# Three-pass down tiles throughout, low parts of the gated products on GpSimd, and an earlier schedule of norm, scores and gates

## The chip, the cores and the metric

One NeuronCore of a Trainium2 chip. The metric is the device time of one execution in microseconds; the kernel before was timed three times.

## The reference, cut to what matters

One layer over 640 rows (512 of a prompt, 8 streams of 16), width 1024: `h = rmsnorm(x)`, one projection `h @ w_in` into nine parts, a width-3 convolution branch and a retention branch of four heads, both gated, `x += m @ w_out`; then `h2 = rmsnorm(x)` and a layer of 16384 single-neuron experts:

```python
q = (hb @ w_q).reshape(PEER_BLOCK, PEER_HEADS, 2, D_HALF)
s = jnp.einsum('thpd,pkd->thpk', q, sk)
sv, si = lax.top_k(s, PEER_TOPK)
...
g = jax.nn.softmax(ts, axis=-1)
a = jax.nn.gelu(jnp.einsum('thkd,td->thk', u_tab[e], hb))
out = jnp.einsum('thk,thkd->td', g * a, v_tab[e])
```

and at the end `x += out` and a last norm.

## The kernel before, in words

The program is one core's, written by hand for each engine: every engine has its own list of instructions in program order, and semaphores tie them. TensorE's order is: turn the normalised rows (`turn_rows`, L1561), 72 products of `w_in` tiles (`product`, L1514 to L1516) with the attention of the head before in between, `w_out` (`by_token`), the query tiles (L1710), 128 up tiles of the expert layer (`up`, L1750) and 128 down tiles (`down_three`, L1807 to L1809, or `down`, L1815).

**Rounded passes.** A float32 product is done in three matmuls of a rounded type (high x high, high x low, low x high) where high and low parts have been made. Of a weight tile ScalarE makes the high part (L692) and GpSimd the low part (`low`, L644). Of the first norm's rows VectorE multiplies by the gain (L1007) and rounds (L1008), and GpSimd makes the low part (`rows_low`, L653); there are two buffers `hf`, one for each half of a block of 128 rows, and TensorE transposes into banks 0 and 1 for every block.

**First norm.** ScalarE squares the five blocks of rows (L736), takes one square root for all; VectorE makes the factors (L984 to L989); ScalarE scales each block (L724); TensorE transposes it; VectorE, GpSimd as above.

**Heads and turns.** Beside the products of `w_in` VectorE also transposes all 128 tiles of `u_t` by 32x32 blocks (`turn`, L1032), so that rows of the up table can be gathered later; SP loads each tile and stores it in four pieces, in the same queue as the `w_in` tiles. In `scores` VectorE multiplies five score tiles by their decay (L1056), scales keys and queries, and turns two u tiles before the fourth score tile; in the first head two more ahead of the first.

**Two ways through the experts.** The first 256 rows are done sparsely: for each of their 128 picks per row one up row and one down row are gathered for all 128 partitions by GpSimd's indirect DMA (L679) into 14 slots, VectorE takes the dot (L1375), ScalarE the gelu and the weight (L894, L900), VectorE adds the weighted down row (L1392). Two picks make a pair (`pair_step`), 128 pairs in all, one dot two pairs ahead. The other 384 rows are done densely: up tiles with gelu, stored as `acts`; gates scattered by one-hot products (`scatter`, L1765) into `gates`; both loaded back in groups of four tiles (`group_in`), multiplied by VectorE (`weigh`, L1426) into `p32`, a ring of four.

**What orders the pairs.** VectorE runs `retrieval(tt)` for five blocks with 9 pairs inside each of the last four (INSIDE), GAP pairs between them, pairs beside the gates, BEFORE_DOWNS pairs, and the rest spread over the down tiles (`pair_after`). `pair_at`, EXP_AT, SCORES_AT, PICKT_AT and GATE_AT are up tiles at which ScalarE and TensorE have their share in their own lists.

**Down tiles.** `three(e)` says which tiles go in three passes: all but e % 8 == 7. For those ScalarE rounds the tile (L947) and the gated product (L949), VectorE makes both low parts (`low_of_tile` L1433, `low_of_gated` L1439). The rings of high and low parts are four tiles deep, that of the loaded tiles eight. TensorE does three 128-row blocks by two halves per tile. GpSimd has only the gathers in this stage; a gather waits until its slot's row of 14 entries ago is used.

Of the kernel before, what the change touches and what calls it, by code (L numbers as in the profile page):

```python
# [72 lines left out]
GAP = 11  # L73
# [12 lines left out]
def pair_at(b):  # L86
# [5 lines left out]
    e = RETRIEVAL_AT + 28.6 * turn + (0.5 + 2.0 * i if i < INSIDE else 17.3 + 0.97 * (i - INSIDE))  # L92
# [7 lines left out]
def three(e):  # L100

    return e % 8 != 7
# [95 lines left out]
def build_program(nc, io):  # L198
    ctx = ExitStack()
    with ctx:  # L200
# [177 lines left out]
        xsT_done = sem("xsT_done")  # L378
        h_split = sem("h_split")
# [85 lines left out]
        def _(sp):  # L465
# [118 lines left out]

            for i in range(3 * A_WQ):
                plain_in(i, io["wq"][i % A_WQ, :, :])
# [4 lines left out]
            def group_in(g):  # L591
                if g >= 2:
                    sp.wait_ge(p_ready, (g - 1) * GROUP)
                if g == 0:
                    for i in range(2):
                        sp.wait_ge(gt_stored[i], 16 * (NB // 2))
                for i in range(2):
                    sp.wait_ge(a_stored[i], 16 * (GROUP // 2) * (g + 1))
                src = gates[g, :, :, :]
                sp.dma_start(gr[:, g % 2, :, :, :].rearrange("p b k t -> p b (k t)"), src).then_inc(g_loaded[g % 2], 16)  # L600
                src = acts[g, :, :, :].rearrange("p k t -> p (k t)")
                sp.dma_start(al[:, g % 2, :, :].rearrange("p k t -> p (k t)"), src).then_inc(al_loaded[g % 2], 16)
# [12 lines left out]
            for u in range(GROUP):  # L615
                down_in(u)
                acts_out(NKEY - GROUP + u)
                if u == 0:
                    group_in(0)
            group_in(1)  # L620
# [18 lines left out]
        def _(pool):  # L639
# [27 lines left out]
            for u in range(GROUP):  # L667
                low(A, u, N_W0 + GROUP + u)
            for n, (kind, r_) in enumerate(ORDER):
                if kind == "u" and r_ % P == 0:  # L670
# [11 lines left out]
                ).then_inc(row_in[n % SLOTS], 16)  # L682


        @block.scalar
        def _(act):
# [44 lines left out]
            for tt in range(TT):  # L731
                act.wait_ge(x_loaded[tt], 16)
                if tt >= 3:
                    act.wait_ge(sum_done, tt - 2)
                bank = 2 + 2 * (tt % 3)
# [1153 lines left out]
```

## Time and profile before

| what | us |
|---|---|
| median of 3 runs | 2223.83 (2220.51 to 2227.95) |
| the profiled execution | 2224.73 |
| its span, first to last instruction | 2222.9 |
| TensorE busy | 2166.9 |
| VectorE busy | 1730.2 |
| GpSimd busy | 866.3 |
| ScalarE busy | 592.8 |
| down stage, first to last matmul | 1670.5 to 2213.9 |

The span is that of the slowest core, here the only one. Busy times of engines overlap. A matmul's recorded length is longer than the distance between two starts, since matmuls are pipelined; distances of starts are used for its cost. The granted clock of TensorE was 0.994 in the mean.

### The profile page before, as it was taken

Reading aid. Unit: us, or ns where it says so; the run is one execution under the profiler, and the core shown is the slowest. Engines: PE = TensorE matmul, PEld = TensorE weight load, DVE = VectorE, ACT = ScalarE, POOL = GpSimd, SP = SyncE. Lnnn points to the kernel's source line nnn. Section 1 sums busy time; section 2 is a strip of 40 time slices with the busy share of each in tenths; the row PEclk is TensorE's granted clock in tenths of the full one; section 3 lists DMA queues with packets and bytes.
Section 4 is the critical chain, followed back from the end, with each engine's and each line's share of the span. In section 5 each row is a group of like instructions: output and inputs, shape, how many; then the busy total and the mean of one; then the engine's idle time right before and its main releaser. Section 6 shows DMA issues by size and latency. Waiting matters only on the chain.

```text
span 2222.9 us, 30818 instructions
## 1 busy us (share of the span) xinstructions
PE 2166.9 (97%) x10473; PEld 1692.8 (76%) x10473; DVE 1730.2 (78%) x3244; ACT 592.8 (27%) x1159; POOL 866.3 (39%) x606
## 2 busy tenths in 40 slices
PE   5999999999999999999999999999999999999998
PEld 5989889899998885655565565577767777777776
DVE  3566675667675285988988989999949898888987
ACT  3212222122223111121221211233324333333333
POOL 4322122223333004576675684512114454454540
PEclk9999999999999999999999999999999999999999
DMA  4999899999983367999999999888899999999993
GB/s 161 304 306 320 288 303 307 318 321 312 309 286 143 108 219 304 355 370 412 403 402 412 389 411 413 337 274 289 292 320 393 413 414 414 413 414 414 414 412 141
DMA packets 314151, 735.40 MB, mean 331 GB/s; under 512 B 30368, under 2 KB 163232, under 8 KB 314016
## 3 DMA queue, kind: packets, MB, share of 16 engines
q1 hardware_dynamic: 189792, 439.67, 54.8%
q0 software_dynamic: 73728, 268.47, 30.6%
q10 hardware_dynamic: 50496, 25.59, 3.8%
q8 instruction: 69, 1.13, 0.2%
q14 instruction: 66, 0.54, 0.1%
HBM read 604.04 MB, written 129.57 MB: 330 GB/s over the span
## 4 chain that ended last, share of the span: by engine, by line
PE 61%; DVE 16%; DMA 7%; issue 6%; POOL 6%; SPq 2%; ACT 1%; DVEq 0%; ACTq 0%; POOLq 0%
PE ps L1750 7%; PE ps L1808 7%; PE ps L1807 7%; PE ps L1809 7%; PE ps L1710 6%; POOL b L679 5%; PE ps L1515 5%; PE ps L1514 5%; DMA b<-in_u_t 5%; PE ps L1516 5%; PE ps L1815 4%; PE ps L1765 3%; DVE b L1392 3%; DMA b<-in_peer_v,b 2%; DVE b L1032 1%
## 5 line engine op out<-in xcount | busy, mean ns | idle before, releaser
L1750 PE MATMUL ps<-b,b 128*128 128x384 f32 x2048 | 665.6, 486 | 0.0
L679 POOL DMA_INDIRECT b<-u_rows,b x256 | 367.2, 1434 | 717.3 <-DVE b L1375 517.9
L1750 PEld LDWEIGHTS ps<-b,b 128*128 128x128 f32 x2048 | 386.8, 190 | 263.4
L644 POOL TENSOR_TENSOR b<-b,b 128x1024 fp32r<-128x1024 f32 x80 | 195.1, 2442 | 468.9 <-ACT b L692 464.4
L1514 PE MATMUL ps<-b,b 128*128 128x320 f32 x1152 | 365.0, 317 | 1.6 <-issue 1.6
L1516 PE MATMUL ps<-b,b 128*128 128x320 f32 x1152 | 357.6, 310 | 0.0
L1515 PE MATMUL ps<-b,b 128*128 128x320 f32 x1152 | 357.5, 310 | 0.0
L1392 DVE SCALAR_TENSOR_TENSOR b<-b,b,b 128x1024 f32<-128x1024 f32 x256 | 330.9, 1292 | 28.3 <-DMA b<-in_peer_v,b 11.2
L1375 DVE CUSTOM_DVE_ANT_0 b<-b,b 128x1024 f32<-128x1024 f32 x256 | 312.5, 1221 | 28.4 <-DMA b<-u_rows,b 22.2
L679 POOL DMA_INDIRECT b<-in_peer_v,b x256 | 291.0, 1137 | 88.6 <-issue 78.3
L1032 DVE STREAM_TRANSPOSE b<-b 128x1024 f32<-128x1024 f32 x128 | 156.9, 1238 | 169.3 <-DMA b<-in_u_t 162.7
L1807 PE MATMUL ps<-b,b 128*128 128x512 f32 x672 | 269.5, 401 | 3.3 <-DVE b L1439 3.3
L1808 PE MATMUL ps<-b,b 128*128 128x512 f32 x672 | 263.2, 392 | 0.0
L1809 PE MATMUL ps<-b,b 128*128 128x512 f32 x672 | 262.1, 390 | 0.0
L1514 PEld LDWEIGHTS ps<-b,b 128*128 128x128 f32 x1152 | 218.0, 189 | 3.0 <-issue 1.9
L1515 PEld LDWEIGHTS ps<-b,b 128*128 128x128 f32 x1152 | 217.8, 189 | 1.0
L1516 PEld LDWEIGHTS ps<-b,b 128*128 128x128 f32 x1152 | 217.6, 189 | 0.0
L884 ACT ACTIVATE b<-ps 128x384 f32<-128x384 f32 x128 | 62.3, 487 | 448.8 <-PE ps L1750 427.8
L707 ACT ACTIVATE b<-ps 128x640 f32<-128x640 f32 (+1 forms) x72 | 50.7, 704 | 423.3 <-PE ps L1516 423.2
L1807 PEld LDWEIGHTS ps<-b,b 128*128 128x128 f32 x672 | 126.4, 188 | 34.9 <-issue 8.0
L1808 PEld LDWEIGHTS ps<-b,b 128*128 128x128 f32 x672 | 126.6, 188 | 30.1 <-issue 4.1
L1433 DVE TENSOR_TENSOR b<-b,b 128x1024 fp32r<-128x1024 f32 x112 | 136.4, 1218 | 14.3 <-ACT b L947 12.4
(164 smaller groups left out, 2588.0 us busy)
## 6 DMA issues: line engine op xcount, KB each, us to landing
b<-in_u_t SPq DMA_DIRECT2D x256, 512.0 KB, 5.5
u_rows<-b SPq DMA_DIRECT2D x512, 128.0 KB, 4.3
b<-in_peer_v SPq DMA_DIRECT2D x128, 512.0 KB
b<-in_w_in SPq DMA_DIRECT2D x72, 512.0 KB
b<-in_wq SPq DMA_DIRECT2D x48, 512.0 KB
acts<-b SPq DMA_DIRECT2D x128, 192.0 KB
gates<-b ACTq DMA_DIRECT2D x12, 2048.0 KB
b<-gates SPq DMA_DIRECT2D x32, 768.0 KB
```

The lines of the kernel that those rows point to most:

```text
L644: nc.gpsimd.tensor_tensor(lo[u][:, :], raw[:, u, :], hi[u][:, :].bitcast(F32), ALU.subtract).then_inc(lo_ready, 1)
L679: nc.gpsimd.indirect_dma_start(slots[n % SLOTS][:, :], None, u_rows if kind == "u" else v_rows, bass.IndirectOffsetOnAxis(ap=row_id[:, r_ ...
L1032: nc.vector.transpose(u_turned[i % 3].rearrange("p (n k j) -> p n k j", n=4, k=KT), u_in[i % 2].rearrange("p (k n i) -> p n k i", k=KT, n= ...
L1375: nc.vector.tensor_tensor_reduce(up_row, up_row, h_row[:, r_ // P, :], 1.0, 0.0, ALU.mult, ALU.add, dots[:, r_ // PAIR % LINES, r_ % PAIR: ...
L1392: nc.vector.scalar_tensor_tensor(token_rows, down_row, row_w[:, b % LINES, i:i + 1], token_rows, ALU.mult, ALU.add).then_inc(row_done, 1)
L1514: nc.tensor.matmul(out, wa_hi[u][:, cols], h_hi[:, k, tok], start=(k == 0), stop=False)
L1515: nc.tensor.matmul(out, wa_hi[u][:, cols], h_lo[:, k, tok], start=False, stop=False)
L1516: last = nc.tensor.matmul(out, wa_lo[u][:, cols], h_hi[:, k, tok], start=False, stop=(k == KT - 1))
L1750: last = nc.tensor.matmul(ps[:, e % 4, 0:TD], w[:, k * P:(k + 1) * P], h2[:, k, SD:T], start=(k == 0), stop=(k == KT - 1))
L1807: nc.tensor.matmul(out, p_hi[:, u, tok], v_hi[n][:, cols], start=(e == 0), stop=False)
L1808: nc.tensor.matmul(out, p_hi[:, u, tok], v_lo[n][:, cols], start=False, stop=False)
L1809: last = nc.tensor.matmul(out, p_lo[:, u, tok], v_hi[n][:, cols], start=False, stop=(e == NKEY - 1))
```

## The change

- `three(e)` is true for every tile; the plain `down` remains in the code and isn't used.
- `low_of_gated` moves from VectorE's list to GpSimd's, placed among the gathers: before a gather whose slot is released by pair b stand all p_lo up to tile `pair_after(b)`.
- First norm: the last two blocks are squared by VectorE (its multiply with a sum, into `yret` as scratch); the rounding moves from VectorE to ScalarE (`rows_high`), each block's behind the scaling of the next; the transposes go to banks 2 to 7 in turn (`norm_bank`); GpSimd's first weight tile stands ahead of the rows.
- `scores`: the turns of u tiles move behind the masks, the first stream keys and the query scaling.
- Schedule: GAP 11 to 10, BEFORE_DOWNS 1 to 6, GATE_AT 99 to 96, the others to match. Group 0 of `acts` is loaded at up tile 124, of `gates` at 126; group 1 behind the first down tile.

```diff
-BEFORE_DOWNS = 1
+BEFORE_DOWNS = 6
+ACTS_AT = 124
+GATES_AT = 126
+SUMS_BY_ACT = 3
...
-EXP_AT = {1: 7, 2: 36, 3: 64, 4: 93}
-SCORES_AT = {2: 6, 3: 45, 4: 73}
-PICKT_AT = {2: 41, 3: 69, 4: 98}
-GATE_AT = 99
+EXP_AT = {1: 7, 2: 35, 3: 62, 4: 90}
+SCORES_AT = {2: 6, 3: 44, 4: 71}
+PICKT_AT = {2: 40, 3: 67, 4: 95}
+GATE_AT = 96
-GAP = 11
+GAP = 10
...
-    return e % 8 != 7
+    return True
...
+def norm_bank(which, tt, b):
+    return b if which else 2 + 2 * (tt % 3) + b
...
@@ sync
+                if e == ACTS_AT:
+                    sp.wait_ge(onehot_used, TD // 4)
+                    acts_in(0)
+                if e == GATES_AT:
+                    for i in range(2):
+                        sp.wait_ge(gt_stored[i], 16 * (NB // 2))
+                    gates_in(0)
...
@@ gpsimd
+            low(A, 0, 0)
             for tt in range(TT):
-                if tt == TT - 2:
-                    low(A, 0, 0)
                 rows_low(0, tt, hf)
...
+            def low_of_gated(e):
+                pool.wait_ge(p_high, SPLIT[e] + 1)
+                u = e % GROUP
+                nc.gpsimd.tensor_tensor(p_lo[:, u, :], p32[:, u, :], p_hi[:, u, :].bitcast(F32),
+                                        ALU.subtract).then_inc(p_split, 1)
+
+            gated = 0
             for n, (kind, r_) in enumerate(ORDER):
+                if n >= SLOTS:
+                    had, r_had = ORDER[n - SLOTS]
+                    b = r_had // PAIR - (AHEAD if had == "u" else 0)
+                    while b >= NPAIR_U and gated < len(THREES) and THREES[gated] <= pair_after(b):
+                        low_of_gated(THREES[gated])
+                        gated += 1
...
@@ scalar
-            for tt in range(TT):
+            for tt in range(SUMS_BY_ACT):
                 act.wait_ge(x_loaded[tt], 16)
...
+            def rows_high(tt):
+                for b in range(2):
+                    act.wait_ge(f_ready, 2 * tt + b + 1)
+                    f = hf[:, b, :].rearrange("p (k t) -> p k t", k=4)
+                    nc.scalar.activation(h_hi[:, 4 * b:4 * b + 4, tt * P:(tt + 1) * P], f, ACT.Copy).then_inc(h_split, 1)
+
+            scale_rows(0, 0, xs)
+            high_a(0, 0, 0, False)
+            for tt in range(1, TT):
                 scale_rows(0, tt, xs)
-                if tt == 1:
-                    high_a(0, 0, 0, False)
+                rows_high(tt - 1)
+            rows_high(TT - 1)
...
@@ vector
-                    line.then(nc.vector.tensor_tensor(f, src, gb, ALU.mult))
-                    nc.vector.tensor_copy(h_hi[hs], f).then_inc(h_split, 1)
+                    nc.vector.tensor_tensor(f, src, gb, ALU.mult).then_inc(f_ready, 1)
+            for tt in range(SUMS_BY_ACT, TT):
+                dve.wait_ge(x_loaded[tt], 16)
+                squares = yret[:, 2 * (tt - SUMS_BY_ACT):2 * (tt - SUMS_BY_ACT) + 2, :].rearrange("p a b -> p (a b)")
+                nc.vector.tensor_tensor_reduce(squares[:, 0:D], x[:, tt, :], x[:, tt, :], 1.0, 0.0, ALU.mult, ALU.add,
+                                               ss[:, tt:tt + 1]).then_inc(sum_done, 1)
...
                 dve.wait_ge(tabs_loaded, g * 48 + 48)
-                if isinstance(g, int) and g == 0:
-                    turn(16, 2)
                 for j in range(PT + 1):
                     if j == 3:
...
-                        turn(0, 2, r, PER_HEAD)
...
+                if isinstance(g, int) and g == 0:
+                    turn(16, 2)
                 for s in range(KW - PT):
                     stream_keys(g, s)
...
+                turn(0, 2, r, PER_HEAD)
...
                 weigh(e)
                 if three(e):
                     low_of_tile(e)
-                    low_of_gated(e)
...
@@ tensor
-                        pe.wait_ge(h_split, rows_from + 2 * TT - 1 + hv)
                         pe.wait_ge(h_ready, rows_from + 2 * -(-(hv + 1) * HALF // P))
...
-                    if tt:
-                        pe.wait_ge(h_ready if which else h_split, which * 2 * TT + 2 * (tt - 1) + b + 1)
+                    if which and tt:
+                        pe.wait_ge(h_ready, which * 2 * TT + 2 * (tt - 1) + b + 1)
+                    if not which and tt >= 3:
+                        pe.wait_ge(f_ready, 2 * (tt - 3) + b + 1)
```

## Rows read from the trace of the kernel before

**Rows 1.** Page, busy us of each engine; the costliest group.
```profile
PE 2166.9 (97%) x10473; PEld 1692.8 (76%) x10473; DVE 1730.2 (78%) x3244; ACT 592.8 (27%) x1159; POOL 866.3 (39%) x606
...
L1750 PE MATMUL ps<-b,b 128*128 128x384 f32 x2048 | 665.6, 486 | 0.0
```

**Rows 2.** Waits of TensorE: engine, line, releaser: us in total, times, longest us.
```profile
PE ps L1633 <- DVE b L1056: 9.0, 3, 3.4
...
PE ps L1743 <- DVE b L1354: 4.5, 2, 3.2
PE ps L1581 <- DVE b L1056: 4.3, 1, 4.3
PE ps L1807 <- DVE b L1439: 3.3, 1, 3.3
```

**Rows 3.** Chain that ended last, and timeline of TensorE (start, us): down stage.
```profile
1700.99 5.15 PE ps L1815 x12
...
2174.79 5.15 PE ps L1815 x12
...
1711.55 0.39 PE L1807 MATMUL ps<-b,b 128*128 128x512 f32 x1
...
1715.63 0.39 PE L1807 MATMUL ps<-b,b 128*128 128x512 f32 x1
```

**Rows 4.** Timeline of all engines, first 34 us.
```profile
10.37 1.00 ACT L736 ACTIVATE ps<-b 128x1024 f32<-128x1024 f32 x1
...
14.58 2.19 ACT L724 ACTIVATE b<-b,b 128x1024 f32<-128x1024 f32 x2 [1.41 <-DVE b L989]
...
15.88 1.94 PE L1561 MATMUL ps<-b,b 128*128 128x128 f32 x8 [15.88 <-ACT b L724]
...
18.31 1.27 POOL L653 TENSOR_TENSOR b<-b,b 128x512 fp32r<-128x512 f32 x1 [17.85 <-DVE b L1008]
...
33.26 0.60 PE L1514 MATMUL ps<-b,b 128*128 128x320 f32 x1 [1.56 <-issue]
```

**Rows 5.** Timeline of VectorE, scores of the second head.
```profile
221.82 1.25 DVE L1032 STREAM_TRANSPOSE b<-b 128x1024 f32<-128x1024 f32 x1 [5.69 <-DMA b<-in_u_t]
222.99 0.67 DVE L1056 TENSOR_TENSOR b<-ps,b 128x128 f32<-128x128 f32 x2
```

**Rows 6.** Timeline of VectorE, end of the first gap between retrievals.
```profile
1008.29 1.23 DVE L1375 CUSTOM_DVE_ANT_0 b<-b,b 128x1024 f32<-128x1024 f32 x1
...
1023.66 1.23 DVE L1375 CUSTOM_DVE_ANT_0 b<-b,b 128x1024 f32<-128x1024 f32 x1
```

**Rows 7.** Down stage: VectorE's timeline and its groups with idle time; a window of all engines.
```profile
1902.80 0.55 DVE L1426 TENSOR_TENSOR b<-b,b 128x384 f32<-128x384 f32 x1
...
1904.40 0.54 DVE L1439 TENSOR_TENSOR b<-b,b 128x384 fp32r<-128x384 f32 x1
...
1907.10 1.22 DVE L1375 CUSTOM_DVE_ANT_0 b<-b,b 128x1024 f32<-128x1024 f32 x1
...
1911.82 0.55 DVE L1426 TENSOR_TENSOR b<-b,b 128x384 f32<-128x384 f32 x1
...
L1426 DVE TENSOR_TENSOR b<-b,b 128x384 f32<-128x384 f32 x126 | 69.1, 550 | 43.6 <-PE ps L1809 30.0 <-PE ps L1815 9.9 <-issue 3.6
...
2000.00:2050.00 50.00, 50.00 (x200) 37.28 (x199) 42.17 (x59) 18.77 (x36) 22.36 (x17) 1.00 1.02 414
```

**Rows 8.** Timelines of VectorE and of GpSimd, rotation of the first head.
```profile
72.47 0.82 DVE L1022 TENSOR_TENSOR b<-b,b 128x640 f32<-128x640 f32 x1
73.33 2.92 DVE L1023 TENSOR_TENSOR b<-b,b 128x640 f32<-128x640 f32 x1
...
73.07 2.50 POOL L644 TENSOR_TENSOR b<-b,b 128x1024 fp32r<-128x1024 f32 x1 [4.63 <-ACT b L692]
```

**Rows 9.** Timeline of GpSimd in the down stage, first and last gather of a pair.
```profile
1899.58 1.73 POOL L679 DMA_INDIRECT b<-u_rows,b  x1 [5.38 <-DVE b L1375]
...
1904.46 1.30 POOL L679 DMA_INDIRECT b<-in_peer_v,b  x1 [0.30 <-issue]
```

More of the change, by code:

```diff
@@ L91, in pair_at @@
     turn, i = b // CYCLE, b % CYCLE
-    e = RETRIEVAL_AT + 28.6 * turn + (0.5 + 2.0 * i if i < INSIDE else 17.3 + 0.97 * (i - INSIDE))
+    e = RETRIEVAL_AT + 27.6 * turn + (0.5 + 2.0 * i if i < INSIDE else 17.3 + 0.97 * (i - INSIDE))
     return math.floor(e)
@@ L378, in build_program @@
         xsT_done = sem("xsT_done")
+        f_ready = sem("normed_rows_turned")
         h_split = sem("h_split")
@@ L583, in acts_out, with acts_in, gates_in, group_in @@
                 sp.dma_start(acts[e // GROUP, :, e % GROUP, :], spill[:, e % 2, :]).then_inc(a_stored[e % 2], 16)
+            def acts_in(g):
+                for i in range(2):
+                    sp.wait_ge(a_stored[i], 16 * (GROUP // 2) * (g + 1))
+                src = acts[g, :, :, :].rearrange("p k t -> p (k t)")
+                sp.dma_start(al[:, g % 2, :, :].rearrange("p k t -> p (k t)"), src).then_inc(al_loaded[g % 2], 16)
+            def gates_in(g):
+                src = gates[g, :, :, :]
+                sp.dma_start(gr[:, g % 2, :, :, :].rearrange("p b k t -> p b (k t)"), src).then_inc(g_loaded[g % 2], 16)
+            def group_in(g):
+                if g >= 2:
+                    sp.wait_ge(p_ready, (g - 1) * GROUP)
+                gates_in(g)
+                acts_in(g)
             for i in range(3 * A_WQ):
@@ L618, in _ @@
                 if u == 0:
[L619 to L620 removed]
+                    group_in(1)
             for u in range(GROUP):
@@ L682, in _ @@
                 ).then_inc(row_in[n % SLOTS], 16)
+            for e in THREES[gated:]:
+                low_of_gated(e)
         @block.scalar
@@ L999, in split_rows @@
                     gb = gain[:, 4 * b:4 * b + 4].unsqueeze(2).broadcast_to([P, 4, P])
-                    src = ps[:, b, :].rearrange("p (k t) -> p k t", k=4)
+                    src = ps[:, norm_bank(which, tt, b), :].rearrange("p (k t) -> p k t", k=4)
                     if which == 1:
@@ L1555, in turn_rows @@
                 for b in range(2):
-                    if tt:
-                        pe.wait_ge(h_ready if which else h_split, which * 2 * TT + 2 * (tt - 1) + b + 1)
+                    if which and tt:
+                        pe.wait_ge(h_ready, which * 2 * TT + 2 * (tt - 1) + b + 1)
+                    if not which and tt >= 3:
+                        pe.wait_ge(f_ready, 2 * (tt - 3) + b + 1)
                     for k in range(4):
                         cols = slice((4 * b + k) * P, (4 * b + k + 1) * P)
-                        last = nc.tensor.transpose(ps[:, b, k * P:(k + 1) * P], xs_[:, tt % 2, cols], ident[:, :])
+                        last = nc.tensor.transpose(ps[:, norm_bank(which, tt, b), k * P:(k + 1) * P], xs_[:, tt % 2, cols],
+                                                   ident[:, :])
                     last.then_inc(xsT_done, 1)
```

21 lines of the change are left out of this document (1 added, 20 removed).

## The prediction

> **What bounds the kernel now.** I read four views. First the page's busy times: TensorE is busy 2166.9 of 2222.9 us [rows 1], so the time is the sum of TensorE's work and of a few places where it stands still. Second, who TensorE waited for: 9.0 and 4.3 us for VectorE's L1056 (masked attention scores), 4.5 us for L1354 (weights of the retrieved rows), 3.3 us for L1439 at the entrance of the down stage [rows 2], and before the first product, which starts only at 33.26 us [rows 4]. Third, the matmuls of the down stage: of every eight tiles seven are done in three rounded passes and one (e % 8 == 7) in plain float32; such a period takes (2174.79 - 1700.99)/14 = 33.84 us [rows 3], and 16 of them, 541.4 us, are a quarter of the run. Fourth, what stands behind TensorE there: VectorE's idle time is little more than the 43.6 us before L1426 in 525 us, and the DMA engines move 414 GB/s at a share of 1.02 [rows 7]. That stage is close to three limits at once, and this decides the case.
>
> **Sum, start of the run.** The profiled execution took 2224.73 us around a span of 2222.9; the sum is made against it, and the median of the three runs, 2223.83, stands 0.9 below.
> - Squares: ScalarE did five blocks one after another, the last at 10.37 [rows 4]; with three left to it and two on VectorE, between 0 (if the last block of x lands that late) and two squares, 2.1 us, are saved. I take the middle, 1.1.
> - Rounding: before, mult and rounding shared VectorE, and from the first scaling (14.58) to the first product (33.26) it was 18.7 us. Now I follow the queues from the first scaling, t. ScalarE: scale 1.1, copy of the first weight tile 1.05; GpSimd starts that tile's low part at t+2.2 and takes about 2.5 (its 1024-wide form, [rows 8]), to 4.7; then six half blocks of 1.27 each [rows 4], with waits of some 0.7 in all on a mult and on the two hf buffers: t+12.9. ScalarE has five scales, the weight copy and six roundings of about 0.6 (half of a 1.1 us scale) ahead of the end of the fifth scale, with its waits t+12.4; the eight transposes (1.94, [rows 4]) end at t+14.4. So the first product starts at t+14.4 and not t+18.7: 4.3 us. The other four halves end at t+18.4, before the product's second half wants them (t+20.8 at the pace at which it starts). Together 5.4 us; bounds 3.5 and 7.
> - The transposes rotate over six banks, so TensorE's wait on the rounding of the block before goes: inside these 5.4.
>
> **Scores ahead of turns.** In the scores of each head VectorE turned two u tiles before the last two masks; the second waited 5.69 us for its load, and the mask started right behind it at 222.99 [rows 5]. TensorE stood for exactly this. With the turns behind the masks and the query scaling, all 9.0 + 4.3 = 13.3 us go. What is moved past: each turn releases a load and four stores on SP's queue, in front of the w_in tiles, by up to 5 us later in the first head (VectorE now waits there for TensorE's last scores). w_in tiles are split two tiles ahead of their use, some 7 us of product each, so I cost that at nothing; without this cover it would give back up to 5 us. Bounds 9 and 13.3.
>
> **Up stage.** GAP 10 in place of 11 takes one pair of rows out of each of three gaps. At the end of a gap VectorE waits for rows: dots start at 1008.29 and, four later, at 1023.66, that is 7.7 us a pair [rows 6]. So picks come 7.7, 15.4 and 23.1 us sooner, and TensorE asks for them 1, 2 and 3 tiles sooner (5.2 us each: 665.6 us of L1750 by 128 tiles, [rows 1]). VectorE gains on it, and the 4.5 us of L1354 go; bounds 0 and 4.5. Gates move with the picks by the same three tiles and stay as VectorE-fed as before: nothing. The five more pairs before the downs (BEFORE_DOWNS 6) fall in time in which VectorE only waited for the last gates and acts to come back: nothing, and the down stage keeps 48 pairs where it had 50. Group 0 loaded sooner gives nothing either: ScalarE rounds the first down tile only behind the last evacuation, and VectorE's queue holds weigh(1) behind the low part of tile 0. At the entrance GpSimd's p_lo takes about 0.96 where VectorE took 0.47: the 3.3 us wait becomes about 3.5.
>
> **Down stage.** Eighteen matmuls of three passes take 1715.63 - 1711.55 = 4.08 us [rows 3]; 128 tiles on TensorE alone are 522.2 us, 19.2 less than 541.4. Can the others follow? Per eight tiles TensorE needs 32.6 us.
> - VectorE: weigh and low tile part 1.60 a tile, a pair 4.72 [rows 7]: 8 x 1.60 + 3 x 4.72 = 27.0. What was removed is 7 p_lo of 0.47, what is added one low tile part of 1.13.
> - But GpSimd and VectorE get in each other's way. A multiply of 0.82 took 2.92 us where GpSimd's subtraction ran from 73.07 for 2.50 [rows 8]: VectorE lost 2.10. For a p_lo of 384 columns GpSimd's length, by the line through 1.27 (512 columns) and 2.50 (1024), is 0.96. VectorE's loss is then 0.56 (0.40 of each instruction does not block), 0.81 (in proportion) or at the worst the whole 0.96. I take 0.70, between the first two: 27.0 + 8 x 0.70 = 32.6.
> - GpSimd: a pair's four gathers run from 1899.58 to 1905.76, 6.2 us [rows 9]; three pairs 18.5, and eight p_lo of 0.96, with a gap of 0.3 and about half a running VectorE instruction (0.5) each, 14.1: 32.6.
> - DMA: a tile brings 0.52 MB of peer_v and 0.39 of gates and acts, a pair 2.10 MB: 13.6 MB at 414 GB/s are 32.9, softened by slots and tiles loaded ahead.
>
> Four queues at the same pace, tied by waits, do not run at the pace of the slowest: GpSimd now holds p_lo(e) behind the gathers of a pair, some 3 us behind VectorE's pair, where VectorE did it at once. I take 33.2 us a period, 531 in all: 10.3 us saved of the 19.2. Bounds: 32.6 (19 saved) and 27.0 + 8 x 0.96 = 34.6 (12 lost).
>
> The Trainium skill ("SBUF — State Buffer", "SBUF: two separate sides") says that the shared ports are held exclusively for the full instruction and the loser fully blocks. By that the loss is the whole 0.96 and the stage the upper bound; the rows show blocking, but 2.10 of 2.50. "GPSIMD Engine Reference" of the Trainium skill (section "Engine selection") advises against two-input elementwise work on GpSimd, about twice as slow; 0.96 beside the 0.55 of L1439 agrees.
>
> **Sum.** 5.4 + 13.3 + 4.5 + 10.3 - 0.2 = 33.3 us off 2224.7: 2191.4, and 0.9 less as a median: 2190.5.
>
> **Rivals.**
> - The port costs its whole length. For: nearly every VectorE instruction of the down stage reads two SBUF tensors, as the blocked one did. Against: 0.4 us of the instruction was not blocked. Stage 554 us; 2224.7 - 23.0 + 12.2 - 0.9 = 2213.
> - GpSimd's queue becomes the bound, slower than before. Place: p_lo(e) queued in order among the gathers. VectorE's instructions of 1.2 us follow one another without gaps, so p_lo may wait a whole one: 0.96 + 0.3 + 1.2 = 2.46 all in; period 18.5 + 19.7 = 38.2, stage 611, time 2271. It decides from (33.84 + 23.0/16 - 18.5)/8 = 2.1 us a p_lo on. Against: in rows 8 GpSimd got in between two back-to-back multiplies, 0.1 us late.
> - The early parts do not reach the end: the delayed SP queue or VectorE's next chain takes the place of the waits of 13.3, and picks stay late. Then some 18 us less: 2208. Against: VectorE idles in the turns, waiting for loads, so it has room.
> - That the change does not do what it says: TensorE's 192 plain instructions are gone by construction; no chance of its own.
>
> **How the numbers follow.** Forecast 0.63, its own range 2180 to 2200; port at full length 0.20; GpSimd's queue 0.07; early parts lost 0.10. The range 2180 to 2214 holds the first, the last and most of the port case. A measurement of this kernel tells 0.3%, about 7 us, from no change, so faster is below 2217 and slower above 2230.5: forecast, early parts lost and half of the port case, 0.83; same 0.08; slower 0.09, the queue and a rest.
>
> **What would show it.** First product near 28 us. No waits of L1633 and L1581 for L1056, none of L1743. In the down stage: 2304 three-pass matmuls, no L1815; period between 32.6 and 33.5; masks of VectorE with single instructions lengthened by some 0.6 to 0.8; small TensorE waits for GpSimd's p_lo in place of none. Wrong if p_lo takes over 1.3 us, if TensorE waits for it over 25 us in all, or if VectorE's idle time before L1426 has gone altogether while TensorE waits for L1433.

## The result, and the profile after

The changed kernel takes 2276.74 us (median of four runs, 2271.28 to 2278.29) where the kernel before took 2225.02 in the same comparison (2220.51 to 2227.95): a ratio of 1.0229, interval 1.0213 to 1.0244. It is slower by 2.3%; forecast was 2190.5. The profiled execution has a span of 2276.5 us, 53.6 more than before.

**Where it went, stage by stage.** The points are starts of TensorE's products in the two traces, the waits are its own; the last column is what the row gave against before, with the term of the forecast beside it.

| point | before | after | gained (forecast) |
|---|---|---|---|
| first product | 33.26 | 28.84 | 4.4 (5.4) |
| up stage starts | 902.7 | 895.3 | 3.0 more (13.3) |
| waits for picks, in all | 4.5 | 0.7 | 3.8 (4.5) |
| last up tile: wait, length | 0, 5.3 | 15.3, 7.4 | -17.4 (0) |
| wait at the entrance | 3.3 | 4.0 | -0.7 (-0.2) |
| down stage starts | 1670.5 | 1677.3 | |
| down stage | 543.4 | 589.1 | -45.7 (+10.3) |
| behind the last product | 9.1 | 10.1 | -1.0 |

The terms of the upper part are 4.4 + 3.0 + 3.8 - 17.4 - 0.7 = -6.9, which is 1677.3 - 1670.5 within a tenth; with the last two rows it is 53.6. (543.4 and 589.1 count from the start of the stage's first product to the end of its last; the prediction's 541.4 is 16 periods of 33.84.)

First the page of the kernel after: busy times, and TensorE, its clock and the DMA rate in 40 slices of 56.9 us each.

```profile
span 2276.5 us, 31118 instructions
...
PE 2168.8 (95%) x10569; PEld 1718.8 (76%) x10569; DVE 1823.1 (80%) x3142; ACT 611.4 (27%) x1197; POOL 1009.3 (44%) x734
...
PE   6999999999999999999999999999969999999897
...
PEclk9999999999999999999999999999989999999999
...
GB/s 196 308 303 311 309 298 305 329 312 316 325 243 39 218 218 371 334 413 412 393 412 390 406 412 318 283 298 290 371 337 359 382 356 383 357 383 359 386 358 132
```

TensorE has almost the busy time of before (2166.9 in [rows 1]), although 192 slow plain products are gone from its work. The down stage has a window of its own (length; busy us of PE, PEld, DVE, ACT and POOL with their instructions; granted clock, DMA share, GB/s):

```profile
1677.30:2266.40 589.10, 546.04 (x2304) 438.39 (x2304) 562.92 (x559) 214.84 (x404) 371.33 (x301) 0.98 0.89 349
```

TensorE is busy 546 us of it, where its 128 tiles need 522.2 by the prediction's 4.08; the other 43 it stands still. Some 14 of the 24 busy us too many are slow clock, by an estimate (eight stretches of 3.4 us at half speed): behind a wait of 2.23 us, for instance, the granted clock was 0.51 for 3.4 us from 1751.8 on, the lower of the two levels (1.2 GHz), with 0.43 us from one product to the next in place of 0.23. VectorE is the bound here: busy 562.9 of 589.1 us, and 25.3 of the rest are waits for ScalarE. In the whole run it grew from 1730.2 to 1823.1 us, although the change took 122 of its instructions away (112 p_lo, 10 roundings) and added 16 low parts of tiles and two squares. From the 31st slice to the 39th the DMA engines move 356 to 386 GB/s, less than the 414 of [rows 7]: they are not the bound of this stage any more.

The waits of TensorE (releaser: us in total, times, longest):

```profile
PE ps L1844 <- POOL b L690: 47.0, 32, 4.0
...
PE ps L1787 <- DMA b<-in_u_t: 15.3, 1, 15.3
PE ps L1637 <- DVE b L1120: 11.5, 4, 4.2
...
PE ps L1780 <- DVE b L1396: 0.7, 1, 0.7
```

Against [rows 2]: the 13.3 us for the masks (L1056) are gone, but L1637 waits 11.5 us for L1120, VectorE's copy of the prompt state. The 4.5 us for picks are 0.7. Two waits are new: one for the load of the last up tile, and 32 for GpSimd's p_lo (L690).

The groups of the down stage, 1677 to 2267 us (busy us, mean ns of one, idle time before):

```profile
L1475 DVE TENSOR_TENSOR b<-b,b 128x1024 fp32r<-128x1024 f32 x127 | 246.2, 1938 | 23.4 <-ACT b L986 23.4
...
L690 POOL TENSOR_TENSOR b<-b,b 128x384 fp32r<-128x384 f32 x128 | 143.2, 1136 | 120.3 <-ACT b L988 119.5
L1417 DVE CUSTOM_DVE_ANT_0 b<-b,b 128x1024 f32<-128x1024 f32 x92 | 137.7, 1497 | 0.0
...
L710 POOL DMA_INDIRECT b<-u_rows,b x85 | 129.7, 1526 | 87.4 <-DVE b L1417 74.6 <-issue 12.8
L1434 DVE SCALAR_TENSOR_TENSOR b<-b,b,b 128x1024 f32<-128x1024 f32 x96 | 125.8, 1311 | 0.2
...
L1468 DVE TENSOR_TENSOR b<-b,b 128x384 f32<-128x384 f32 x127 | 75.8, 597 | 0.0
```

The instruction to look at is L1475, VectorE's low part of a down tile: 1938 ns on average. Three of them, with what GpSimd did beside them (timelines of VectorE and of GpSimd; start, length):

```profile
1909.05 1.21 DVE L1475 TENSOR_TENSOR b<-b,b 128x1024 fp32r<-128x1024 f32 x1
...
1911.28 3.37 DVE L1475 TENSOR_TENSOR b<-b,b 128x1024 fp32r<-128x1024 f32 x1 [0.54 <-ACT b L986]
...
1915.04 1.21 DVE L1475 TENSOR_TENSOR b<-b,b 128x1024 fp32r<-128x1024 f32 x1
1916.17 2.04 DVE L1417 CUSTOM_DVE_ANT_0 b<-b,b 128x1024 f32<-128x1024 f32 x1
...
1911.57 1.99 POOL L690 TENSOR_TENSOR b<-b,b 128x384 fp32r<-128x384 f32 x2
1915.75 1.38 POOL L690 TENSOR_TENSOR b<-b,b 128x384 fp32r<-128x384 f32 x1 [2.20 <-ACT b L988]
```

The same subtraction takes 1.21 us with GpSimd on its gathers and 3.37 us beside two p_lo of 1.99 together: VectorE lost 2.16, as much as GpSimd used. GpSimd lost nothing (two of 0.995). Even the fact that VectorE's instruction had started 0.29 us earlier didn't protect it. The third case is milder: a single p_lo that starts 0.71 us into L1475 leaves it its 1.21, takes 1.38 itself, and the next VectorE instruction takes 2.04 for 1.21. Of the 128 p_lo, 86 stand in 43 pairs such as the second case, with 2.15 us lost by VectorE for a pair on average, and 42 are alone as in the third, with 0.82 lost.

The second new wait starts on SP's queue (its timeline, and TensorE's):

```profile
1659.48 0.32 SPq L602 DMA_DIRECT2D b<-gates  x1
1659.84 0.43 SPq L588 DMA_DIRECT2D b<-in_u_t  x1
...
1665.92 7.40 PE L1787 MATMUL ps<-b,b 128*128 128x384 f32 x16 [15.26 <-DMA b<-in_u_t]
1677.34 0.77 PE L1844 MATMUL ps<-b,b 128*128 128x512 f32 x1 [4.03 <-POOL b L690]
```

The load of group 0 of `gates` now stands ahead of the last u tile in SP's queue, and it waits for the last store of `gates`. That store was issued at 1615.20 us and landed only 44.2 us later; before it took 13.7 us (issued at 1642.11, its group loaded from 1655.9). The last u tile waited behind it, and TensorE behind that. The tile then took 7.40 us, where others take some 5.3 (5.2 by [rows 1], and the end of the last product); the slice of the page in which it lies (the 30th) is the one with a granted clock of 0.8 in place of 0.9 and more, and over the tile itself it was 0.73.

### The profile page after: what moved, and what is told of

The parts are those of the page before. It is cut to its first block, busy times and chain, and to the rows that moved or that the text cites. A ratio compares the mean times of both kernels' runs of the same rounds, so it can differ in the third digit from the quotient of the medians.

```text
span 2276.5 us, 31118 instructions
## 1 busy us (share of the span) xinstructions
PE 2168.8 (95%) x10569; PEld 1718.8 (76%) x10569; DVE 1823.1 (80%) x3142; ACT 611.4 (27%) x1197; POOL 1009.3 (44%) x734
## 3 DMA queue, kind: packets, MB, share of 16 engines
q10 hardware_dynamic: 50496, 25.59, 3.7%
## 4 chain that ended last, share of the span: by engine, by line
PE 43%; DVE 24%; issue 11%; DMA 9%; POOL 8%; ACT 2%; SPq 2%; DVEq 0%; ACTq 0%
POOL b L710 7%; PE ps L1787 6%; PE ps L1747 6%; DVE b L1434 6%; PE ps L1548 5%; PE ps L1549 5%; PE ps L1550 5%; DMA b<-in_u_t 4%; PE ps L1802 3%; PE ps L1844 3%; DVE b L1417 3%; PE ps L1845 3%; PE ps L1846 3%; DMA b<-in_peer_v,b 2%; DMA gates<-b 2%
## 5 line engine op out<-in xcount | busy, mean ns | idle before, releaser
L1787 PE MATMUL ps<-b,b 128*128 128x384 f32 x2048 | 667.9, 487 | 15.3 <-DMA b<-in_u_t 15.3
L1787 PEld LDWEIGHTS ps<-b,b 128*128 128x128 f32 x2048 | 388.0, 191 | 279.7 <-DMA b<-in_u_t 15.9
L1434 DVE SCALAR_TENSOR_TENSOR b<-b,b,b 128x1024 f32<-128x1024 f32 x256 | 332.5, 1299 | 35.8 <-ACT b L939 19.1
L1417 DVE CUSTOM_DVE_ANT_0 b<-b,b 128x1024 f32<-128x1024 f32 x256 | 338.3, 1322 | 23.5 <-DMA b<-u_rows,b 21.7
L1844 PE MATMUL ps<-b,b 128*128 128x512 f32 x768 | 307.9, 401 | 47.0 <-POOL b L690 47.0
L1845 PE MATMUL ps<-b,b 128*128 128x512 f32 x768 | 305.3, 397 | 0.0
L1846 PE MATMUL ps<-b,b 128*128 128x512 f32 x768 | 304.0, 396 | 0.0
L1475 DVE TENSOR_TENSOR b<-b,b 128x1024 fp32r<-128x1024 f32 x128 | 247.4, 1933 | 33.8 <-ACT b L986 33.7
L1548 PEld LDWEIGHTS ps<-b,b 128*128 128x128 f32 x1152 | 219.3, 190 | 1.2
L1549 PEld LDWEIGHTS ps<-b,b 128*128 128x128 f32 x1152 | 219.2, 190 | 1.2
L1550 PEld LDWEIGHTS ps<-b,b 128*128 128x128 f32 x1152 | 218.8, 190 | 0.0
L1844 PEld LDWEIGHTS ps<-b,b 128*128 128x128 f32 x768 | 146.9, 191 | 92.8 <-issue 61.9
L690 POOL TENSOR_TENSOR b<-b,b 128x384 fp32r<-128x384 f32 x128 | 143.2, 1136 | 120.3 <-ACT b L988 119.5
L1846 PEld LDWEIGHTS ps<-b,b 128*128 128x128 f32 x768 | 147.3, 192 | 32.0
## 6 DMA issues: line engine op xcount, KB each, us to landing
b<-in_peer_v SPq DMA_DIRECT2D x128, 512.0 KB, 12.3
```

The source lines that it names most:

```text
L1417: nc.vector.tensor_tensor_reduce(up_row, up_row, h_row[:, r_ // P, :], 1.0, 0.0, ALU.mult, ALU.add, dots[:, r_ // PAIR % LINES, r_ % PAIR: ...
L1434: nc.vector.scalar_tensor_tensor(token_rows, down_row, row_w[:, b % LINES, i:i + 1], token_rows, ALU.mult, ALU.add).then_inc(row_done, 1)
L1475: nc.vector.tensor_tensor(v_lo[n % HALVES][:, :], down_tile(e), v_hi[n % HALVES][:, :].bitcast(F32), ALU.subtract).then_inc(v_split, 1)
L1548: nc.tensor.matmul(out, wa_hi[u][:, cols], h_hi[:, k, tok], start=(k == 0), stop=False)
L1549: nc.tensor.matmul(out, wa_hi[u][:, cols], h_lo[:, k, tok], start=False, stop=False)
L1550: last = nc.tensor.matmul(out, wa_lo[u][:, cols], h_hi[:, k, tok], start=False, stop=(k == KT - 1))
```

## The experiments

The first theory, formed from these rows: all that is new in the down stage comes from **where p_lo is computed** (VectorE blocked for GpSimd's whole instruction, and ScalarE's rounding uncovered), while the three-pass tiles themselves save what they should; and 5 us come from the early load of group 0. Rivals: GpSimd's queue (p_lo among the gathers) is late by itself; the DMA rate; the tiles.

**1. p_lo back on VectorE**, all else as changed.

```diff
@@ gpsimd
-                nc.gpsimd.tensor_tensor(p_lo[:, u, :], p32[:, u, :], p_hi[:, u, :].bitcast(F32),
-                                        ALU.subtract).then_inc(p_split, 1)
...
@@ vector, behind each tile's low part
+                nc.vector.tensor_tensor(p_lo[:, u, :], p32[:, u, :], p_hi[:, u, :].bitcast(F32),
+                                        ALU.subtract).then_inc(p_split, 1)
```

> The changed kernel with the low parts of the gated products back on VectorE; everything else as changed, 128 tiles in three passes. Theory 1 (the port): VectorE loses the whole length of each of GpSimd's subtractions (1.0 us x 128) and then waits for ScalarE's rounding of the tile; without them VectorE needs 128 x (1.60 + 0.47) + 48 x 4.72 = 492 us, TensorE 522, so the down stage falls from 590 to about 527 and the time to 2214 (2207 to 2222). The forecast's theory for the rest (four queues at one pace): 2214 too. Rival (three passes in all tiles, or the DMA's load, are what costs): the stage stays above 560, time above 2245.

Measured: 2211.97 us, 0.993 of before (0.9908 to 0.9952), 64.8 below the changed kernel. The groups of its down stage, 1674 to 2202 us:

```profile
L1460 DVE TENSOR_TENSOR b<-b,b 128x1024 fp32r<-128x1024 f32 x127 | 154.9, 1220 | 20.9 <-ACT b L971 17.8
...
L1419 DVE SCALAR_TENSOR_TENSOR b<-b,b,b 128x1024 f32<-128x1024 f32 x96 | 124.3, 1294 | 0.2
L1402 DVE CUSTOM_DVE_ANT_0 b<-b,b 128x1024 f32<-128x1024 f32 x92 | 112.1, 1219 | 0.0
...
L1453 DVE TENSOR_TENSOR b<-b,b 128x384 f32<-128x384 f32 x127 | 69.6, 548 | 3.0 <-PE ps L1838 3.0
```

And a window of all engines (busy us of PE, PEld, DVE, ACT and POOL with their instructions, then granted clock, DMA share and GB/s):

```profile
1700.00:2150.00 450.00, 450.00 (x1982) 371.84 (x1981) 427.12 (x577) 190.00 (x343) 215.95 (x164) 1.00 1.02 414
```

One edit restores the stage: TensorE never stands from 1700 to 2150, the low part is 1220 ns again, the stage takes 1674.4 to 2201, some 527 us (forecast for TensorE alone: 522.2). These means are also the measure of what was lost: L1475 (1938 - 1220) x 127 = 91.2 us, L1417 (1497 - 1219) x 92 = 25.6, L1468 (597 - 548) x 127 = 6.2, L1434 17 x 96 = 1.6, together 124.6, or **0.98 us for each p_lo**, whose own shortest length is 0.995. It is a mean of the two kinds above: 1.07 a p_lo where two go through together, 0.82 where one is alone.

**2. Group 0 loaded as before**, p_lo left on GpSimd.

```diff
-                if e == ACTS_AT:
-                    sp.wait_ge(onehot_used, TD // 4)
-                    acts_in(0)
-                if e == GATES_AT:
-                    for i in range(2):
-                        sp.wait_ge(gt_stored[i], 16 * (NB // 2))
-                    gates_in(0)
...
@@ behind the last up tile
+                    for i in range(2):
+                        sp.wait_ge(gt_stored[i], 16 * (NB // 2))
+                    group_in(0)
```

> The changed kernel with group 0 of acts and gates loaded where it was before, behind the first down tile. Theory A (SP's queue): the wait for the stored gates stood ahead of the last u_t load; the 15.3 us of TensorE before the last up tile go, 17 us with the slow clock behind it. Theory B (the gates' store is itself late, 44 us after its issue, because five more pairs of gathers compete with it): the 15.3 us go but TensorE then waits for the first gates at the entrance; the gain is only 5 to 10 us, time 2267 to 2272.

Measured: 2271.66 us, 1.020 (1.0171 to 1.023); 5.1 below the changed kernel. The largest wait of TensorE:

```profile
PE ps L1840 <- POOL b L686: 58.3, 28, 17.8
```

The stall of 15.3 ahead of the last up tile is gone, and one of 17.8 at the entrance has come: the down stage needs the same late gates. The early load only moved the wait to the front and made one tile slow; what is really late is the store.

**3. Both edits together.**

> Both edits of the two runs above together. If they are separate costs the gains add: 2276.7 - 63 - 8 = 2206 (2198 to 2214), faster than the kernel before. Rival (the costs overlap): not below e1_plo_vector by more than 2 us.

Measured: 2207.37 us, 0.9907 (0.988 to 0.9934). The four corners are 2276.7, 2212.0 (p_lo moved back), 2271.7 (loads moved back), 2207.4 (both): p_lo is worth 64.8 and 64.3 us, the loads 5.1 and 4.6. The two are independent. The loads' 5 us are near the noise: with p_lo on GpSimd the runs overlap (2271.28 to 2278.29 against 2270.32 to 2274.91), with p_lo on VectorE they don't (2211.00 to 2215.77 against 2206.74 to 2210.58). This version beats both kernels.

**4. Only p_lo on GpSimd, in the kernel before** (its 112 three-pass tiles): the edit of experiment 1 the other way round.

> The kernel before with only the low parts of the gated products moved to GpSimd (112 tiles, placed by the same rule), nothing else. Theory 1: VectorE's 52 us of idle time are eaten: it was occupied 473 us of 525, gives up 52, takes on 112 x 1.0 of blocked time and some 27 of waits for ScalarE, so the stage grows by about 33 us, time 2258 (2248 to 2266). My forecast's price (0.70 a piece, no waits for ScalarE): 2225, no change.

Measured: 2246.35 us, 1.0088 (1.006 to 1.0116). Its groups, 1671 to 2230 us:

```profile
L1448 DVE TENSOR_TENSOR b<-b,b 128x1024 fp32r<-128x1024 f32 x109 | 214.0, 1963 | 19.1 <-ACT b L962 19.0
...
L1407 DVE SCALAR_TENSOR_TENSOR b<-b,b,b 128x1024 f32<-128x1024 f32 x100 | 135.5, 1355 | 0.2
L1390 DVE CUSTOM_DVE_ANT_0 b<-b,b 128x1024 f32<-128x1024 f32 x96 | 133.6, 1392 | 0.0
```

The blocking is there without anything else of the change, about the same for each p_lo (some 109 us for 112, 0.97 each). The time grew by 19 us and not by 65, since here TensorE needs 33.84 us for eight tiles. By the prediction's durations VectorE's work in that time is 27.0, less one low tile part of 1.13, with 50 pairs in place of 48 0.6 more, 7 p_lo of 0.97, and 19.0/16 = 1.2 of waits for ScalarE (6.8 in all before): 34.4, so some 10 us more over 16 periods; the stage grew by 18.4 (from 543.4 to 561.8, 1666.5 to 2228.3). Most of the rest is that those durations come out 8 us short: VectorE was busy 500.0 us in the stage of experiment 1, where they give 492. My 2258 was 12 too high, just outside its own range.

**5. A memset in the place of the subtraction**: same queue, same waits, same 384 columns written by GpSimd, nothing read. It leaves the low parts of the gated products zero.

```diff
-                nc.gpsimd.tensor_tensor(p_lo[:, u, :], p32[:, u, :], p_hi[:, u, :].bitcast(F32),
-                                        ALU.subtract).then_inc(p_split, 1)
+                nc.gpsimd.memset(p_lo[:, u, :].bitcast(F32), 0.0).then_inc(p_split, 1)
```

> The changed kernel with GpSimd's subtraction replaced by a memset of the same 384 columns: the low parts of the gated products are left out (zeros), the queue, its order and its waits stay. If VectorE is held up by what GpSimd's instruction reads and writes over its whole length, VectorE's instructions are back at 1.21 us or lengthened only by the memset's own length, and the stage falls to 540 or less (time under 2230). If it is the place in GpSimd's queue behind the gathers, TensorE still waits for GpSimd some 40 us and the time stays above 2255.

Measured: 2214.61 us in one run. VectorE's low part of a tile (groups, 1677 to 2205 us):

```profile
L1474 DVE TENSOR_TENSOR b<-b,b 128x1024 fp32r<-128x1024 f32 x128 | 156.3, 1221 | 74.1 <-ACT b L985 73.9
```

and GpSimd's memset, by its line (shortest/median/longest ns, first and last start):

```profile
L690 POOL MEMSET b<- x128: 417/433/445, 1677.2 to 2188.9; 128x384 f32 x128
```

This separates the theory from the rival of the queue. The memset stands at the same place among the gathers, waits for the same roundings, and is 433 ns long; TensorE never waited for it, VectorE's 1221 ns show nothing of it, and the stage is some 525 us. The place in the queue costs nothing; the blocking comes with an instruction that reads SBUF. (The memset is also shorter, 0.43 for 1.0 us, but even those 0.43 lengthened nothing. Whether a GpSimd instruction with one input would block as one with two does, no run shows.) VectorE had 74 us of waits for ScalarE here and still kept up. The Trainium skill ("SBUF — State Buffer", "SBUF: two separate sides") says that a VectorE instruction with two SBUF inputs contends only with a GpSimd instruction that reads SBUF, and that the loser is blocked for the whole of it. The memset's run agrees with the first; with the second the 2.16 us lost to 1.99 of GpSimd agree, and the 0.82 lost to a single p_lo of 1.0 are less.

**6. ScalarE rounds tile e+1 ahead of the gated product e**, p_lo left on GpSimd. Before, ScalarE took tile e's rounding only behind the gated product e-1, and VectorE's p_lo had filled part of that time.

```diff
+                    tile_high(0)
+                if e + 1 < NKEY:
+                    tile_high(e + 1)
+                act.wait_ge(p_ready, e + 1)
+                nc.scalar.activation(p_hi[:, e % GROUP, :], p32[:, e % GROUP, :], ACT.Copy).then_inc(p_high, 1)
...
-                act.wait_ge(p_ready, e + 1)
-                nc.scalar.activation(p_hi[:, e % GROUP, :], p32[:, e % GROUP, :], ACT.Copy).then_inc(p_high, 1)
```

> The changed kernel with one edit on ScalarE: it rounds down tile e+1 before the gated product of tile e, so that VectorE finds the rounded tile ready. If VectorE is the bound of the down stage and its 33.7 us of waits for ScalarE's rounding (L986) count in full, they go and the stage falls from 590 to about 558, time 2245 (2240 to 2252). If GpSimd's queue (L690) is the bound, TensorE goes on waiting for it and the time stays within 8 us of 2276.

Measured: 2227.43 us, 0.9999 (0.9986 to 1.0011): 49.3 below the changed kernel, more than expected. Its groups, 1677 to 2217 us:

```profile
L1481 DVE TENSOR_TENSOR b<-b,b 128x1024 fp32r<-128x1024 f32 x127 | 179.6, 1414 | 0.0
L1423 DVE CUSTOM_DVE_ANT_0 b<-b,b 128x1024 f32<-128x1024 f32 x92 | 148.5, 1614 | 0.0
L1440 DVE SCALAR_TENSOR_TENSOR b<-b,b,b 128x1024 f32<-128x1024 f32 x96 | 137.3, 1430 | 0.2
L1474 DVE TENSOR_TENSOR b<-b,b 128x384 f32<-128x384 f32 x126 | 97.5, 774 | 0.0
```

VectorE's wait for ScalarE fell from 33.7 to 10.4 us, and these 10.4 are one wait that ends ahead of the stage's first product; inside the stage 23.4 went to nothing. The lengthening is 24.6 + 36.3 + 13.1 + 28.5 = 102.5 us by the means of experiment 1, or 0.81 for each p_lo instead of 0.98. The timelines of VectorE and of GpSimd:

```profile
1911.69 1.36 DVE L1474 TENSOR_TENSOR b<-b,b 128x384 f32<-128x384 f32 x1
1912.98 2.04 DVE L1481 TENSOR_TENSOR b<-b,b 128x1024 fp32r<-128x1024 f32 x1
1914.94 2.03 DVE L1423 CUSTOM_DVE_ANT_0 b<-b,b 128x1024 f32<-128x1024 f32 x1
...
1911.47 4.42 POOL L690 TENSOR_TENSOR b<-b,b 128x384 fp32r<-128x384 f32 x3
```

Where VectorE has its next instruction ready, the two engines take turns: three p_lo in a row take 4.42 us where alone they take 3.0, and each VectorE instruction loses 0.81 to 0.83. In the changed kernel each of the 43 instructions hit by two p_lo had waited some 0.54 us for ScalarE, and there GpSimd went through at its own pace. (Such an instruction is also less far on when p_lo starts, 0.29 against 0.71 us; which of the two decides is not shown.) So ScalarE's wait cost twice: 23 us of its own and 22 of blocking. That is 45 of the 49.

**7. Only the three-pass tiles, in the kernel before.**

```diff
 def three(e):
-    return e % 8 != 7
+    return True
```

> The kernel before with only the 16 plain down tiles made three-pass; the low parts stay on VectorE, the schedule as before (50 pairs beside the down tiles). TensorE's work alone falls by 19.2 us. VectorE takes on 16 x (1.13 + 0.47) = 26 us against 52 us of idle time; the DMA engines have 128 tiles of 0.92 MB and 50 pairs of 2.10 MB less what is loaded ahead. By e3_both_back (48 pairs, stage 525 us) and e5_one_pair_before (53 pairs, 549 us, VectorE waiting for rows) 50 pairs should stand at 530 to 535: time 2217 (2210 to 2220). If TensorE alone decided: 2208.

Measured: 2217.14 us, 0.9952 (0.9932 to 0.9972), the down stage 1676.5 to 2207.2, 531 us. Its start is 6 us later than before, with picks a little later (TensorE's wait for them 7.5 for 4.5 us), which took part of the 12.7 that the stage gained. Alone, this line of the diff is worth 10 us; what else experiment 3 has of the change (first norm, scores, schedule, six pairs before the downs) is worth the other 10.

**8. One pair of rows before the downs, not six** (on top of experiment 3). I supposed that the extra gathers delay the gates' store.

```diff
-BEFORE_DOWNS = 6
+BEFORE_DOWNS = 1
```

> e3_both_back with BEFORE_DOWNS back at 1, so that no block of five more pairs of gathers runs while the last gates are stored. Theory: the store's 512-byte pieces share the DMA engines with the rows' 4 KB pieces and landed 45.8 us after their issue; without those gathers it lands in under 16 us, TensorE's 17.4 us at the entrance fall to about 4, VectorE needs 128 x 2.07 + 53 x 4.72 = 515 us beside TensorE's 522: time 2194 (2189 to 2200). Rival: the store is late because the gates end too close to the downs, or VectorE becomes the bound in the down stage: time stays above 2203.

Measured: 2215.92 us, 0.9947 (0.9928 to 0.9966): 8.5 slower than experiment 3. Half of the theory held. The stores' and loads' time to landing (tile `gates`, 1600 to 1650 us; the longest is the store's):

```profile
DMA to landing us min/median/max: 5.9/9.8/13.7
```

VectorE's waits for rows in its down stage:

```profile
DVE b L1415 <- DMA b<-in_peer_v,b: 15.1, 12, 1.7
DVE b L1398 <- DMA b<-u_rows,b: 3.7, 4, 1.5
```

and its window:

```profile
1700.00:2150.00 450.00, 438.40 (x1900) 358.94 (x1898) 427.83 (x577) 178.19 (x341) 225.96 (x176) 0.99 1.02 414
```

The store takes 13.7 us again and the down stage starts at 1655.4 in place of 1672.6, 17 us sooner. But it ends at 2203.3 in place of 2198.7: five more pairs to gather in a stage whose DMA engines already move 414 GB/s. The rows come late, and TensorE waits 18.2 us, in ten places, for the low parts behind them.

**9. Three pairs before.**

```diff
-BEFORE_DOWNS = 6
+BEFORE_DOWNS = 3
```

> e3_both_back with BEFORE_DOWNS 3 in place of 6 (51 pairs beside the downs). Two costs trade: the gates' store lands earlier with fewer gathers beside it (45.8 us at six, 13.7 at one), and each pair moved beside the downs costs the DMA engines 5.1 us there. Entrance wait about 8 us, stage about 536: time 2208 (2202 to 2213), no better than either end. If only the entrance counted: 2198.

Measured: 2207.01 us, 0.9908 (0.9885 to 0.9931), as six pairs. The store takes 29.3 us, the stage starts at 1658.5 and ends at 2198.2.

**10. Six pairs, but GpSimd holds the gathers until the last gates are stored** (on top of experiment 3).

```diff
+            held = []
...
+                    b = r_had // PAIR - (AHEAD if had == "u" else 0)
+                    if b >= NPAIR_R + BESIDE_HOTS + 1 and not held:
+                        held.append(n)
+                        for i in range(2):
+                            pool.wait_ge(gt_stored[i], 16 * (NB // 2))
```

> e3_both_back with one wait on GpSimd: the gathers that follow the second of the six pairs ahead of the downs wait until the last gates are stored. If the store is late because of these gathers (and not because of the pairs' place as such), it lands in about 15 to 20 us, TensorE's 17.4 us at the entrance fall to about 4 and the down stage keeps its 525 us with 48 pairs: time 2195 (2190 to 2200). If the held gathers make VectorE late for the first down tile instead, it stays above 2203.

Measured: 2206.48 us, 0.9911 (0.9893 to 0.9929): within the spread of experiments 3 and 9, and not the 2195 that I expected. The waits of TensorE in its down stage:

```profile
PE ps L1838 <- DVE b L1468: 12.5, 9, 8.2
```

and its window:

```profile
1700.00:2150.00 450.00, 447.24 (x1955) 365.24 (x1954) 421.23 (x569) 185.30 (x337) 213.34 (x162) 1.00 1.02 414
```

The store takes 13.6 us, so the gathers had slowed it; the stage starts at 1660.5, 12 us sooner than in experiment 3, and ends at 2194.6, 4 us sooner. The four versions start at 1655.4, 1658.5, 1660.5 and 1672.6 and end at 2203.3, 2198.2, 2194.6 and 2198.7, all with the DMA engines at 414 GB/s. The end no longer follows the start. That the bytes left to move set it is what the windows suggest; I have not tried it with fewer bytes.

**11. Only the order of the scores, in the kernel before**, the two turns behind the masks and the query scaling.

```diff
-                if isinstance(g, int) and g == 0:
-                    turn(16, 2)
...
+                if isinstance(g, int) and g == 0:
+                    turn(16, 2)
```

> The kernel before with only the turns moved behind the masks in the scores. The 13.3 us of TensorE's waits for L1056 go, but VectorE's later step (the copy of the prompt state) takes their place with 9 to 12 us; the up stage starts 1 to 3 us sooner (before 902.7). By my forecast it would start 13 us sooner.

Measured: 2222.41 us in one run, its up stage at 897.0 where before it was 902.7. TensorE's waits, whole run:

```profile
PE ps L1600 <- DVE b L1078: 10.4, 4, 3.5
PE ps L1743 <- DVE b L1354: 8.2, 2, 6.9
```

The 13.3 us of [rows 2] become 10.4 for the next item of VectorE's chain, the copy of the prompt state, and still the up stage starts 5.7 us sooner; the first head alone gives 7.4 (first product of L1600 at 142.1 for 149.5), more than its wait of 4.3. Behind that wait the granted clock of the kernel before was 0.50 for 3.4 us (from 124.4 on; half speed costs 1.7 there), and 0.3 come from the start; about 1 stays open. In the up stage most of it is lost: TensorE waits 8.2 us for the picks (4.5 before), and the down stage starts 0.7 us sooner. Picks come by VectorE's and the DMA's schedule, not by TensorE's; in the changed kernel, with GAP 10, the wait for them is 0.7 (GAP was not changed alone).

**12. Key rotation behind the prompt state** (on top of experiment 3), to clear that new wait.

```diff
-                rotate_k(h)
...
+                rotate_k(h)
```

> e3_both_back with VectorE's rotation of the keys of the next head behind the copy of the prompt state (L1120 in the changed kernel) and the first stream's state, for which TensorE waited 11.5 us. If that order is the cause, these 11.5 us go and the time is 2196 (2193 to 2200); if the waits only move to a later step of VectorE's chain, it stays within 4 us of 2207.

Measured: 2206.99 us, 0.99 (0.988 to 0.9921), nothing gained over 2207.37. TensorE's waits in the scores:

```profile
PE ps L1599 <- DVE b L1120: 8.2, 3, 3.0
PE ps L1625 <- DVE b L1101: 4.1, 1, 4.1
```

They are 12.3 us in place of 11.7. The wait follows VectorE's chain as a whole, whichever item stands first.

## Why the prediction was wrong

**The down stage** failed, by 56 of the 86 us between forecast (2190.5, its range up to 2214) and result, and the step is "**I take 0.70**, between the first two". It measured 0.98 a p_lo, 36 us over 128 of them. The bounds were at hand (0.56, 0.81, 0.96), and the working said that in the worst case the whole length is lost; the top was right and I weighed it at one in five. I had one row with 2.10 of 2.50 and carried its unblocked 0.4 us over to shorter instructions, as a length or in proportion. It can't be carried over: the same p_lo cost 1.07 or 0.82 us within one stage, and experiment 6 shows that the mean falls to 0.81 when VectorE finds its next instruction ready.

The second failed step is one that isn't in the sum: **what the 0.47 us p_lo covered**. VectorE's own p_lo had stood between the gated product e-1 and the low part of tile e, just where ScalarE rounded tile e. With it gone VectorE waited 23.4 us for ScalarE inside the stage. The clean pair is the kernel before and experiment 4, where only p_lo moved: 6.8 and 19.0. By the working of the prediction, a period of eight tiles is then 27.0 + 8 x 0.98 + 23.4/16 = 36.3 us, and 16 of them 581; measured 589.1. The missing 8 are those by which 1.60 a tile and 4.72 a pair are short (experiment 4). My 33.2 had neither the whole price nor the waits; it had 0.6 a period for four queues instead.

Against this, "What was removed is 7 p_lo of 0.47" was right in itself and worthless as a saving: 0.47 us on VectorE were exchanged for 0.98 blocked on it. With p_lo left on VectorE, 8 x (1.60 + 0.47) + 3 x 4.72 = 30.7 us a period, it stays below TensorE's 32.6. **TensorE's term was right**: 4.08 us a tile, 522.2 in all; experiment 1 gave 527 with TensorE always busy. "Four queues at the same pace" was never put to the test: in the changed kernel VectorE alone was the bound, and in experiment 1 VectorE and GpSimd had room (busy 500.0 and 229.2 us of 526.7).

**The rivals.** "The port costs its whole length" had the mechanism; its 554 us stage missed ScalarE's wait, its 2213 that and the stall below. "GpSimd's queue becomes the bound" gave 2271, close to the result and wrong: GpSimd was idle for 120.3 + 87.4 us of the stage, its p_lo took 1.14 on average, some 1.4 with the gap of 0.3, and not the 2.1 all in at which that rival decides, and experiment 5 left it in place and lost the delay. A rival's number coming out isn't its proof. Of the prediction's own signs of being wrong, one came: TensorE waited for p_lo 47.0 us in all, over the 25 named.

**"Group 0 loaded sooner gives nothing"** was right of a gain and blind to a loss: 15.3 us of stall and 2.1 of a slow tile; against the entrance wait that it replaces it cost 5 us (experiments 2 and 3). The prediction asked what the load would bring and not what is queued behind its wait: there stood the last u tile. **The five more pairs, "nothing" in the prediction,** were wrong in the same place: they slow the gates' store from 13.7 to 45 us (experiments 8 to 10). In exchange they take bytes out of a stage whose DMA engines move 414 GB/s, and six pairs were 8.5 us better than one, and no better than three.

**Scores ahead of turns**, "all 9.0 + 4.3 = 13.3 us go": those waits did go, but 11.5 us came for the next thing on VectorE's queue. Together with the rest of the early stages it brought 3.0 us. The bounds of 9 to 13.3 were no bounds, as they held only if nothing of VectorE's was late behind the masks. The rival "early parts lost" was right for this term.

**Start**: 4.4 of 5.4. The squares saved nothing. VectorE's first waited for x until 9.27 and the second followed at 10.54, so the first scaling began at 14.86 and not at 13.5 (timelines of VectorE and ScalarE):

```profile
10.54 1.23 DVE L1050 CUSTOM_DVE_ANT_0 b<-b 128x1024 f32<-128x1024 f32 x1
...
14.86 1.15 ACT L757 ACTIVATE b<-b,b 128x1024 f32<-128x1024 f32 x1 [1.41 <-DVE b L1028]
```

From there to the first product it is 13.98 us; the working gave 14.4 for 18.7 of before. **Picks**: 3.8 of 4.5, as forecast. **Entrance**: 4.0 us, 3.5 forecast.

## What to carry to other kernels

A subtraction given to GpSimd is not off VectorE's account while VectorE works on two SBUF tensors: price it at its full length on both engines, and move it only if that is shorter than what VectorE needs itself (here 0.98 for 0.47). When an instruction leaves an in-order queue, ask what finished behind its back. And a load that waits for a store is put behind everything that doesn't need the store, in the queue where it stands.

## What was new in the hardware

- GpSimd's two-input instruction of 384 columns took 0.995 us at least and took 0.98 on average from VectorE's instructions with two SBUF inputs, even from one that had started 0.29 us before; in experiment 6, where VectorE had the next instruction ready, the two took turns, and each lost: VectorE 0.81, GpSimd 0.37 (1.397 on average for 1.02). GpSimd's memset of the same columns (0.433 us) lengthened nothing. Nor did its subtractions lengthen VectorE's transpose, which has one input: in the kernel before 40 that ran beside them and 74 that didn't both took 1.24 us on average.
- A store of 2 MB in pieces of about 500 bytes took 13.3 to 14.4 us with the gathers of one pair or none ahead of the downs, and 29.3 to 45.9 with those of three or six, in pieces of about 3.6 KB. The sizes come from the page of the kernel after (packets, MB, share of 16 engines; q0 are the gathers, q10 the store's queue):

```profile
q0 software_dynamic: 73728, 268.47, 30.5%
q10 hardware_dynamic: 50496, 25.59, 3.7%
```

25.59 MB in 50496 pieces are 507 bytes each. The Trainium skill ("DMA: Bandwidth & Descriptors", "Queues, rings and completion order") says that each DMA engine goes round its queues packet by packet; by that a queue of small pieces would get a small share of the bytes. The 13.7 and 45.8 us agree with it, but no run changed the size of the pieces.
